# A PEER expert layer on one core: where the gates leave PSUM, and how many U blocks run ahead of the expert loop

## The reference

```python
def peer_ffn(h, w_q, sub_k1, sub_k2, expert_u, expert_v):
    ...
    v1, i1 = lax.top_k(s1, PEER_TOPK)
    v2, i2 = lax.top_k(s2, PEER_TOPK)
    ...
    vals, pos = lax.top_k(cand, PEER_TOPK)
    experts = jnp.take_along_axis(cand_idx, pos, axis=-1)
    gates = jax.nn.softmax(vals, axis=-1)
    ...
        u = expert_u[ec]
        a = jnp.einsum('cd,chkd->chk', xc, u).astype(jnp.float32)
        w = (jax.nn.gelu(a) * gc).astype(xc.dtype)
        return jnp.einsum('chk,chkd->cd', w, expert_v[ec])
```

## Time and profile before

| | us |
|---|---|
| median of 3 runs | 1760.5 (1760.37 to 1760.77) |
| the profiled execution | 1760.59 |
| its span | 1758.8 |
| PE busy in it | 1703.6 (97%) |
| VectorE busy | 1345.5 (76%) |
| ScalarE busy | 999.4 (57%) |
| GpSimd busy | 417.1 (24%) |

### The profile page before, as it was taken

How to read it: one execution, slowest core, us unless ns; L and a number is a source line. 1 busy time by engine, 2 the same in 40 slices (tenths; PEclk the granted TensorE clock), 3 DMA queues, 4 the chain that set the end, 5 groups by cost and what they waited for, 6 DMA issues and landing times.

```text
span 1758.8 us, 29551 instructions
## 1 busy us (share of the span) xinstructions
PE 1703.6 (97%) x10408; PEld 1499.8 (85%) x10408; DVE 1345.5 (76%) x2599; ACT 999.4 (57%) x1629; POOL 417.1 (24%) x186
## 2 busy tenths in 40 slices
PE   9999999969999999999999999999999999999998
PEld 8997999958888888888888888877899988989996
DVE  7658759977777777777888887876769975769974
ACT  6578654536666666653333333566566645556653
POOL 1220177747777767620000000000000000000000
PEclk9999999989999999999999999999999999999999
DMA  7661555546666666677777788653465564535562
GB/s 308 203 228 50 192 180 190 186 129 194 195 194 195 189 197 188 193 243 241 240 240 243 243 309 291 230 198 130 146 202 194 195 205 157 180 120 192 192 203 73
DMA packets 120449, 346.45 MB, mean 197 GB/s; under 512 B 13328, under 2 KB 45200, under 8 KB 118928
## 3 DMA queue, kind: packets, MB, share of 16 engines
q1 hardware_dynamic: 118480, 336.70, 58.7%
q10 hardware_dynamic: 1856, 8.23, 1.3%
HBM read 321.03 MB, written 23.86 MB: 196 GB/s over the span
## 4 chain that ended last, share of the span: by engine, by line
PE 81%; DVE 13%; ACT 5%; issue 1%; DMA 0%; ACTq 0%; DVEq 0%
PE bank L866 79%; DVE wsplit L2723 3%; DVE bank L2718 2%; DVE hot_a L2721 2%; DVE gates L2731 1%; ACT wsplit L1959 1%; DVE pick L2632 1%; PE bank L1270 1%; DVE act_e L2709 1%; DVE ropeg L2709 1%; ACT gates L2023 0%; DVE pick L2615 0%; ACT act_e L2026 0%; ACT ropeg L2026 0%; ACT wsplit L1672 0%
## 5 line engine op out<-in xcount | busy, mean ns | idle before, releaser
L866 PE MATMUL bank<-HT,wsplit 128*128 128x256 f32 (+1 forms) x5292 | 756.0, 303 | 1.3 <-POOL wsplit L1649 0.6
L866 PEld LDWEIGHTS bank<-HT,wsplit 128*128 128x128 f32 x5292 | 700.2, 189 | 49.1 <-issue 3.4
L1959 ACT ACTIVATE wsplit<-raw 128x1024 fp32r<-128x1024 f32 x252 | 266.7, 1058 | 212.8 <-PE bank L866 209.1
L866 PE MATMUL bank<-wsplit,wexp 128*128 128x512 f32 x1536 | 348.3, 389 | 0.0
L866 PEld LDWEIGHTS bank<-wsplit,wexp 128*128 128x128 f32 x1536 | 288.3, 188 | 59.7
L1649 POOL TENSOR_TENSOR wsplit<-raw,wsplit 128x1024 fp32r<-128x1024 f32 x124 | 299.6, 2417 | 142.5 <-ACT wsplit L1959 142.4
L1672 ACT ACTIVATE wsplit<-raw 128x1024 fp32r<-128x1024 f32 x146 | 154.3, 1059 | 97.4 <-PE bank L866 96.3
L2141 DVE TENSOR_TENSOR wsplit<-raw,wsplit 128x1024 fp32r<-128x1024 f32 x124 | 151.5, 1234 | 68.4 <-ACT wsplit L1672 67.2
L2703 DVE TENSOR_TENSOR wsplit<-raw,wsplit 128x1024 fp32r<-128x1024 f32 x128 | 156.0, 1219 | 1.0 <-ACT wsplit L1959 1.0
L2141 DVE TENSOR_TENSOR wsplit<-raw1b,wsplit 128x1024 fp32r<-128x1024 f32 x101 | 121.4, 1220 | 40.0 <-ACT wsplit L1672 39.5
L1672 ACT ACTIVATE wsplit<-raw1b 128x1024 fp32r<-128x1024 f32 x102 | 107.6, 1059 | 72.7 <-PE bank L866 68.4
(11 more groups left out here) (321 smaller groups left out, 2010.7 us busy)
## 6 DMA issues: line engine op xcount, KB each, us to landing
raw<-weights SPq DMA_DIRECT2D x148, 512.0 KB, 4.2
raw<-expert_v SPq DMA_DIRECT2D x128, 512.0 KB, 3.6
raw<-expert_u SPq DMA_DIRECT2D x124, 512.0 KB, 3.7
raw1b<-weights SPq DMA_DIRECT2D x102, 512.0 KB, 4.2
raw1a<-weights SPq DMA_DIRECT2D x48, 512.0 KB, 4.4
HT<-acts_parked SPq DMA_DIRECT2D x124, 128.0 KB, 3.4
acts_parked<-act_e SPq DMA_DIRECT2D x62, 128.0 KB, 3.7
acts_parked<-ropeg SPq DMA_DIRECT2D x62, 128.0 KB, 3.7
```

The source lines that it names most:

```text
L866: ins = pe.matmul(out, lhsT, rhs, start=start, stop=stop, **kw)
L1959: act.activation(wsplit[:, s, 0, :], src, ACT.Copy).then_inc(e_hi, 1)
```

## The change

Three edits. EARLY goes from 12 to 20, and HOT_SPAN from 112 to 104: eight more blocks of U are multiplied ahead of the choice's end, the loop has 108 blocks in place of 116, and the 64 groups are spread over 104 of them, 1.625 blocks apart. Banks 4 to 7 become two pairs, a group's four tokens have one pair, and `gates_out` and its ScalarE copy are one instruction of 512 elements in place of two of 256; each walks over the four tokens first (neighbours in `gates`, 1 KB apart in PSUM) and over the 128 blocks second. In VectorE's slot m, `add_halves(m)` comes ahead of `gates_out`, where it came behind. The copy of the iota row moves from behind early block 8 to behind early block 12.

```diff
-EARLY = 12
+EARLY = 20
-FIRST_HOT, HOT_SPAN = 2, 112
+FIRST_HOT, HOT_SPAN = 2, 104
-        PS = [ctx.enter_context(nc.psum_tensor(f"bank{b}", [P, 512], F32)) for b in range(8)]
+        PS = [ctx.enter_context(nc.psum_tensor(f"bank{b}", [P, 512], F32))[:, :] for b in range(4)]
+        wide_banks = [ctx.enter_context(nc.psum_tensor(f"banks{b}_{b + 1}", [P, 2, 512], F32)) for b in (4, 6)]
+        PS += [pair[:, n, :] for pair in wide_banks for n in range(2)]
...
-            return [PS[4 + (2 * g + n) % 4] for n in range(2)]
-        def gates_of(g, n):
-            at = TOGETHER * g + 2 * n
-            return gates[:, :, at:at + 2].rearrange("p i t -> p t i")
-        def hot_halves(b):
-            return b[:, :].rearrange("p (t b n) -> p t b n", t=2, b=2)
+            return [wide_banks[g % 2][:, n, :] for n in range(2)]
+        def gates_of(g):
+            return gates[:, :, TOGETHER * g:TOGETHER * (g + 1)]
+        def hot_half(g, half):
+            return wide_banks[g % 2][:, :, :].rearrange("p w (t b n) -> p b n (w t)", t=2, b=2)[:, half]
...
-                    pe.wait_ge(hot_out, 2 * (g - 1))
+                    pe.wait_ge(hot_out, g - 1)
...
-                if n == 8:
+                if n == 12:
                     act.wait_ge(norm_d, KD * (TURNS.index("mem1") + 1))
                     act.activation(iota_bank, iota, ACT.Copy).then_inc(iota_made, 1)
...
                     act.wait_ge(hot_full, g + 1)
-                    for half, b in enumerate(hot_banks(g)):
-                        act.activation(gates_of(g, half), hot_halves(b)[:, :, 1, :], ACT.Copy).then_inc(hot_lo, 1)
+                    act.activation(gates_of(g), hot_half(g, 1), ACT.Copy).then_inc(hot_lo, 1)
...
-                for n, b in enumerate(hot_banks(g)):
-                    dve.wait_ge(hot_lo, 2 * g + n + 1)
-                    dve.tensor_tensor(gates_of(g, n), hot_halves(b)[:, :, 0, :], gates_of(g, n), ALU.add).then_inc(hot_out, 1)
+                dve.wait_ge(hot_lo, g + 1)
+                dve.tensor_tensor(gates_of(g), hot_half(g, 0), gates_of(g), ALU.add).then_inc(hot_out, 1)
...
             for m in range(BULK):
+                add_halves(m)
                 for g in hot_groups_at(m):
                     gates_out(g)
-                add_halves(m)
                 for g in hot_groups_at(m + FIRST_HOT):
                     make_hots(g)
```

More of the change, by code:

```diff
@@ L1513, in _ @@
                 times_u(m)
-            pe.wait_ge(hot_out, 2 * HOT_GROUPS)
+            pe.wait_ge(hot_out, HOT_GROUPS)
             for e in range(4):
@@ L2756, in _ @@
                 if m == BULK - 3:
-                    dve.wait_ge(hot_out, 2 * HOT_GROUPS)
+                    dve.wait_ge(hot_out, HOT_GROUPS)
                     second_part(0, 0)
```

## The result

| | before | changed |
|---|---|---|
| median of the runs, us | 1760.55 | 1767.78 |
| lowest to highest, us | 1759.87 to 1760.77 | 1765.92 to 1771.94 |
| span of the profiled execution, us | 1758.8 | 1766.4 |

The ratio is 1.0047, with a 95% interval of 1.0034 to 1.0060: slower by 7.2 us. The changed kernel's runs also spread over 6.0 us, where those of before keep within 0.9.

A forecast was written before the change was run, and what follows sets the result against it. PE idles before the expert transposes, waiting for pick; a VectorE chain closes the loop's long intervals. Transposes +15.7, clock -1.2, shorter loop -28.9, moved add +24.6 make +10.2 on 1760.59: 1770.8 us, range 1761 to 1783.

The forecast's parts named there:

- the likeliest case: VectorE and GpSimd alternate, add 0.61 to 0.7 us, expert transposes between 384.2 and 389.9: 1766.7 to 1776 us, 62%.
- the sum: Whole kernel, against 1760.59 us: +15.7 - 1.2 - 28.9 + 24.6 = +10.2, so 1770.8 us.
- The moved add: Main loop: gates_out between add_halves and make_hots delays PE in 39 long intervals, 0.63 us each, 24.6 us (23.8 to 50.3).
- The row of the VectorE reduce: Profile row: 512 elements at 1 KB PSUM steps take 0.683 us, full speed; taken as evidence for a cheap gates' add.
- The shorter loop: Main loop: 64 groups in 102 blocks, 24 short and 39 long intervals, 345.4 us; 28.9 us shorter.
- The turns: End of early blocks: two-SBUF-input VectorE instructions alternate with GpSimd subtractions; expert transposes (et) move from 371.82 to 387.5, +15.7 us.
- The rule behind the turns: End of pick: VectorE and GpSimd are locked for whole instructions, the later blocking fully; said to give the 387.5 us.
- The clock behind et: After the expert transposes: PE, no longer idle 15.9 us, should be nearer full clock; 1.2 us back, at most 2.1.

The follow-up runs named there:

- The small GpSimd rows above: Changed kernel with GpSimd making only the first 16 of 1024 columns of the lo parts of U blocks 15 to 22: 1759.6 us.
- the one with 16: Changed kernel with add_halves behind gates_out again, EARLY 16 and HOT_SPAN 108: 1754.5 us, ratio 0.9965.

## Why the prediction was right

1770.8 us was forecast, 1767.8 measured; the sign and the likeliest case were right. Between the profiled executions 10.2 us were forecast and 7.6 measured. The 2.6 us between them are these: et came 1.6 us earlier than forecast, the clock behind it gave back 0.8 less, the loop was 1.3 shorter, and 0.5 was saved behind the loop, for which the sum had no term.

- **The moved add** was put at 39 x 0.63 = 24.6 us. It is 39 x 0.60 = 23.4 us by the chain, and 22.6 by taking it back. The row of the VectorE reduce decided rightly about the 1 KB steps in PSUM: the add is 0.681 us for 512 elements, the duration of a contiguous one in the earlier trace rows. The Trainium skill ("PSUM — Partial Sum Buffer", Specifications) says that PSUM has 8-byte lines and that an access pattern that isn't contiguous slows matmuls. The trace shows, with these 0.681 us, that this doesn't carry over to this VectorE read.
- **The shorter loop** was put at 28.9 us, down to 345.4. With the old order and 20 early blocks the trace has 345.8 us from the first to the last product (394.71 to 740.51), against 345.4 counted.
- **The turns** were put at et 387.5; it was 385.9, inside the bounds of 384.2 to 389.9. The mechanism is as described, with two details off. GpSimd took the first turn, ahead of L2637 (363.24 to 365.65), which the sum had given to VectorE. And it took about a turn less at the end: ScalarE's split of block 21 waited 1.36 us for its transfer, which the sum had not counted, so that L2645 met one subtraction, not two, and L2686 waited for the last 1.2 us of one. VectorE's 10.1 us in the sum leave out L2684 and L2685 (0.42 and 0.25 us); in the trace they ran beside the last subtraction. The order of the first turn differs between kernels that are alike up to there: in the changed kernel with the old order L2637 went first (363.18, 4.42 us). PE was to wait ahead of blocks 16 to 19; it waited only ahead of block 17 (1.86 us), took 10.82 us for the last three blocks, at a granted clock of 0.72 from 372 to 378, and ended at 383.1, where 384.2 was counted.
- **The rule behind the turns.** The Trainium skill ("SBUF — State Buffer", Who interferes with whom) gave what no row of before could show, that the later of the two waits for the whole instruction. The small GpSimd rows above agree: 2.34 us for an instruction of 0.22.
- **The clock behind et** was to give back 1.2 us and gave 0.4. PE waited 2.81 us before et. The six transposes themselves took 0.87 us in place of 1.54, but the first two blocks behind them took 7.38 us, where they had taken 7.24, and the granted clock was 0.83 in the window from 385 to 395. This is the smallest term and the one that was wrong in its reason: it was assumed that a short wait leaves the clock up.
- **The spread** of 6 us between the runs had no place in the forecast. It may be that the wait before et varies with the turns, and the clock behind it with the wait. The traces fit that: a wait of 0.92 us and 5.82 us for the two blocks with the old order, 2.81 and 7.38 in the changed kernel. The other kernels bear it out only in part. Where GpSimd takes no turns, or where et has no wait ahead of it (28 and 44 early blocks), the runs lie within 1.7 us. Of the others two spread as widely as the changed kernel (6.4 us in the old order, 5.8 with `make_hots` in front), but the kernel before with 20 early blocks (1.8) and the one with 16 (1.5) do not. No two runs of one kernel were profiled, so the cause stays open.

## What to carry to other kernels

Before work is moved in an engine's queue, look at the chain that closes the loop and count what stands between its ends: an instruction of 0.6 us was free on one side of `add_halves` and cost 23 us on the other. The same chain showed the larger gain, since `make_hots` needs nothing of the block that it was queued behind. And work that fills an engine's hole brings its helpers along: eight blocks that fitted PE's hole brought GpSimd into the way of the VectorE work that the hole was waiting for.

## What the runs showed of the hardware

- VectorE and GpSimd exclude each other for whole instructions when VectorE reads two tensors from SBUF, in both directions: a bf16 multiply of 4.43 us took 6.63, and a GpSimd subtraction of 0.22 us took 2.34. Where one of VectorE's two inputs lies in PSUM, neither was lengthened: in the loop of the changed kernel L2723 took 1.215 us in all 64 cases, one of them (751.39 to 752.61) wholly inside a GpSimd subtraction (750.24 to 752.62) of the usual 2.38 us.
- With a wait of 1.85 us in each long interval PE's granted clock over the loop was 0.88 to 0.89, with 1.13 us it was 1.00. So 0.60 us more in the chain of 47 intervals cost 28 us, and 1.33 us more cost 116, in place of the 64 that the longer intervals account for.
- Behind a wait of 2.81 us and the transposes two blocks took 7.38 us; behind 2.16 us they took 7.23 and 7.36 (in two kernels), behind 0.92 they took 5.82, and behind none 5.84.
- A VectorE add or ScalarE copy of 512 float32 that steps 1 KB in PSUM and writes runs of four to SBUF costs as much as a contiguous one (0.68 and 0.60 us), where runs of one, 1 KB apart in SBUF, had made 256 elements cost 0.77 and 0.66.
